# Halo sums on GpSimd, a claim per residual tile, idle matmuls in TensorE's planned waits, and new tune values, in a hybrid decoder block on eight cores

## The reference

```python
h = rmsnorm(x, norm_mix)
u_pool, u_rnn, u_gate, g_pool, g_rnn = split(h @ w_in)      # 512, 1024, 1024, 1024, 1024 columns
y_pool = (pool_mixer(u_pool) * scale) @ w_pool_out           # trailing windows 2/4/8/16, 4 groups of 128
v = causal_depthwise_conv(u_rnn, conv_w, conv_b)             # width 4: y_t = b + sum_k w[k] u_(t-3+k)
r, i = sigmoid(v @ w_a + b_a), sigmoid(v @ w_x + b_x)        # block-diagonal, 8 heads of 128
a = exp(-8 r softplus(-lam))
hr = scan(h_t = a_t h_(t-1) + sqrt(1 - a_t^2) i_t v_t)       # along the sequence
y_rnn = (hr * gelu(u_gate)) @ w_rnn_out
x = x + (sigmoid(g_pool) * y_pool + sigmoid(g_rnn) * y_rnn) @ w_o
g, u = split(rmsnorm(x, norm_ffn) @ w_ffn_in)                # 2816 each
out = rmsnorm(x + (silu(g) * u) @ w_ffn_out, norm_final)
```

## Time and profile before

| | us |
|---|---|
| median of 3 runs | 1113.86 |
| lowest and highest run | 1113.6, 1180.95 |
| the profiled execution | 1112.0 |
| its span, core 6 (slowest) | 1110.4 |
| even cores (role 0) | 1104.9 to 1110.4 |
| odd cores (role 1) | 1074.1 to 1080.5 |

### The profile page before, as it was taken

The page is one execution under the profiler, slowest core; times in us unless marked ns, Lnnn a source line. Parts: engine busy times, 40 slices in busy tenths (PEclk is TensorE's granted clock), DMA queues, the critical chain, the costliest instruction groups (busy, mean ns, idle before and its releaser), DMA issues.

```text
span 1110.4 us, 18573 instructions; the slowest of 8 cores (1074.1 to 1110.4 us)
## 1 busy us (share of the span) xinstructions
PE 995.2 (90%) x4720; PEld 444.9 (40%) x4720; DVE 727.9 (66%) x840; ACT 473.7 (43%) x602; POOL 257.5 (23%) x394
## 2 busy tenths in 40 slices
PE   3996679998879998798999999979999799999996
PEld 2442234443334443343444444434444344444442
DVE  4569777588997547987658989893633433334336
ACT  3476764256645216656228747761211110110112
...
GB/s 219 178 137 75 109 113 212 209 192 143 67 23 151 151 58 48 67 69 127 91 169 117 125 86 214 214 147 152 61 145 152 99 114 36 77 104 25 109 39 155
DMA packets 64914, 132.65 MB, mean 119 GB/s; under 512 B 7200, under 2 KB 11680, under 8 KB 64800
## 3 DMA queue, kind: packets, MB, share of 16 engines
...
...
## 4 chain that ended last, share of the span: by engine, by line
PE 72%; DVE 13%; issue 8%; ACT 4%; DMA 1%; POOL 1%; DVEq 0%; SPq 0%; ACTq 0%; POOLq 0%
PE ps L815 52%; PE ps L1160 13%; DVE f_v_f L857 4%; PE ps L1105 3%; PE ps L760 2%; PE ps L885 2%; DVE R_f L857 1%; DVE f_v_f L862 1%; DMA X<-x 1%; DVE R_f L941 1%; DVE f_w_f L928 1%; POOL rs_f L750 0%; PE ps L1029 0%; DVE ACW_f L857 0%; ACT hbt_f L744 0%
## 5 line engine op out<-in xcount | busy, mean ns | idle before, releaser
L815 PE MATMUL ps<-H_f,ring_f 128*128 128x512 bf16 x2816 | 649.0, 387 | 31.2 <-DVE uh_f L866 8.4
L815 PEld LDWEIGHTS ps<-H_f,ring_f 128*128 128x128 bf16 x2816 | 274.2, 99 | 385.9 <-issue 86.5
L1135 ACT ACTIVATE th_f<-ps 128x512 f32<-128x512 f32 (+1 forms) x66 | 48.7, 739 | 225.1 <-PE ps L815 220.0
L1160 PE MATMUL ps<-ACW_f 128*128 128x512 bf16 x528 | 116.4, 379 | 0.0
L676 POOL DMA_DIRECT2D ring_f<-w_ffn_in x88 | 47.3, 538 | 288.7 <-PE ps L815 244.0
L1139 DVE SCALAR_TENSOR_TENSOR th_f<-th_f,ps 128x512 f32<-128x512 f32 (+1 forms) x66 | 57.0, 864 | 80.0 <-ACT th_f L1135 62.7
L857 DVE SCALAR_TENSOR_TENSOR f_v_f<-ps,par,f_v_f 128x511 f32<-128x511 f32 (+5 forms) x90 | 89.6, 996 | 25.2 <-ACT f_v_f L852 16.6
L748 POOL TENSOR_SCALAR ms_f<-ms_f 128x1 f32<-128x1 f32 x64 | 23.5, 367 | 244.2 <-ACT hbt_f L744 241.6
L1045 ACT ACTIVATE th_f<-ps 128x512 f32<-128x512 f32 (+1 forms) x48 | 35.2, 738 | 101.8 <-PE ps L815 93.8
L1160 PEld LDWEIGHTS ps<-ACW_f 128*128 128x128 bf16 x528 | 51.4, 98 | 61.5 <-issue 0.4
L1166 DVE SCALAR_TENSOR_TENSOR X<-ps,X 128x1024 f32<-128x1024 f32 x36 | 43.9, 1223 | 41.9 <-PE ps L1160 37.3
...
## 6 DMA issues: line engine op xcount, KB each, us to landing
...
```

Source lines behind the costliest of these rows:

```text
L815: it.add(c_pe(n), lambda e, kc=kc, lo=lo, n=n, b=b: e.matmul(PS[pv.idx // 2][:, pv.idx % 2 + b, 0:n], lhsT=ring[:, w.idx, kc, :], rhs=src[ ...
L1135: it.add(c_act(U), lambda e, U=U, pg=pg, tv=tv: e.activation(out=two(th[:, tv.idx, 0:U], U), in_=P2(pg, U), func=AF.Tanh, scale=0.5), (pg, ...
L1160: it.add(c_pe(), lambda e, c=c, i=i: e.matmul(PS[pv.idx // 2][:, c, :], lhsT=acs[i][0](t * 128, (t + 1) * 128), rhs=WA[:, i, c * 512:(c + ...
```

## The change

Four edits:

1. The last three columns of u are now copied into `uh` by ScalarE, ahead of v = w3 u + b in the same item. When the units of four channel blocks of a segment are done with that, `halo_terms` computes on GpSimd, in three instructions for the four blocks, the three sums that the next segment's first three columns need (`hc`), from a table of taps in the parameters; the conv item of a later segment adds them in one VectorE instruction over 3 columns instead of three products.
2. A residual load of segment c1b claims the rows of R that its tile covers (two), and not all eight.
3. After the schedule is laid out, each TensorE item that starts a new PSUM value at least `keep` = 1.0 us after TensorE's last item (by the plan, and after 60 us) gets one matmul of 512 columns ahead of it, and one more per item of the chain that it waits for, at least 0.8 us apart, each waiting for that item's end. They write the PSUM bank of the item that follows, whose own first matmul starts the bank anew.
4. New tune values for both roles.

```diff
--- before.py
+++ after.py
@@ -32,16 +32,16 @@
         self.tune = tune
-TUNE0 = {"seq": "g0 g1 c01 g23 g45 c23 c45 g67 c67", "nc0": -3.85, "nc0s": 3.0, "step": 24.05, "gelu": 4.32,
-         "halo": 43.21, "pool": 25.05, "pools": 0.39, "t1": 93.39, "t1s": 1.88, "B0": 73.78, "S0": 285.6,
-         "B1": 386.59, "S1": -3.62, "B2": 589.89, "S2": 304.97, "ahead": 22.26, "c1": 1.278, "m": 37.56, "f": 7.53,
-         "u": 7.799, "slack": 0.098, "dev": 2, "hs": 20.8, "devt": 2, "pvo": 1, "pvt": 4, "pmo": 3, "pmt": 0,
-         "pbo": 0, "pbt": 2, "pao": 1, "pat": 0}
-TUNE1 = {"seq": "p0 p1 p23 g01 c01 p45 g23 c23 p67 g45 c45 g67 c67", "nc0": 11.68, "nc0s": 3.0, "step": 20.24,
-         "gelu": 3.77, "halo": 34.0, "pool": 45.93, "pools": 7.44, "t1": 183.82, "t1s": -0.44, "B0": 154.25,
-         "S0": 122.17, "B1": 334.63, "S1": -4.81, "B2": 394.66, "S2": 261.45, "ahead": -59.77, "c1": 0.565,
-         "m": 29.63, "f": 14.85, "u": 2.664, "slack": 0.121, "dev": 0, "hs": 20.01, "devt": 2, "pvo": 4, "pvt": 1,
-         "pmo": 1, "pmt": 0, "pbo": 4, "pbt": 0, "pao": 4, "pat": 3}
+TUNE0 = {"seq": "g0 g1 c01 g23 g45 c23 c45 g67 c67", "nc0": -1.38, "nc0s": 1.59, "step": 24.94, "gelu": 5.29,
+         "halo": 41.1, "pool": 24.03, "pools": 2.81, "t1": 98.04, "t1s": 3.77, "B0": 74.11, "S0": 276.71,
+         "B1": 384.25, "S1": -3.62, "B2": 668.36, "S2": 300.6, "ahead": 22.0, "c1": 1.249, "m": 37.56, "f": 7.38,
+         "u": 2.841, "slack": 0.086, "dev": 1, "hs": 20.8, "devt": 2, "pvo": 1, "pvt": 2, "pmo": 1, "pmt": 0,
+         "pbo": 0, "pbt": 0, "pao": 0, "pat": 0, "keep": 1.0}
+TUNE1 = {"seq": "p0 p1 p23 g01 c01 p45 g23 c23 p67 g45 c45 g67 c6 c7", "nc0": 11.68, "nc0s": -1.2, "step": 22.79,
+         "gelu": 1.4, "halo": 34.0, "pool": 47.28, "pools": 7.44, "t1": 236.41, "t1s": -0.44, "B0": 201.28,
+         "S0": 122.17, "B1": 334.63, "S1": -4.1, "B2": 394.66, "S2": 245.88, "ahead": -59.66, "c1": 0.611,
+         "m": 35.5, "f": 14.85, "u": 1.297, "slack": 0.121, "dev": 0, "hs": 21.04, "devt": 1, "pvo": 4, "pvt": 1,
+         "pmo": 0, "pmt": 0, "pbo": 2, "pbt": 0, "pao": 0, "pat": 1, "keep": 1.0}
 ROLES = (
     Role(0, (), 1024, ((1024,), (1024,)), (512, 512), 512, 5, (4, 4, 4, 4), (8, 8, 8, 8), (4, 2, 4, 2), True, 3, 4, True, TUNE0),
@@ -53,7 +53,8 @@
 C_CW, C_CB, C_BA, C_BX, C_LAM, C_PS, C_INV = 0, 32, 40, 48, 56, 64, 68
-C_N = 68 + 64
+C_HALO = 68 + 64
+C_N = C_HALO + 72
 class _Op:
@@ -498,6 +499,8 @@
         one_t = sb("one_t", [128, 1])
         hs_t = sb("hs_t", [128, 8])
         uh = sb("uh", [128, 8, 3])
+        hx = sb("hx", [128, 4, 3, 3])
+        hc = sb("hc", [128, 8, 3])
         ph = sb("ph", [128, 4, 16])
         hst = sb("hst", [128, 8])
         NSS = 8
@@ -602,14 +605,15 @@
         XR = R[:, :, :].rearrange("p k n -> p (k n)").bitcast(F32)
         ACP = PM[:, :, :].rearrange("p k n -> p (k n)")[:, 0:8 * NB].rearrange("p (m n) -> p m n", m=8)
-        RALL = [("R", j, q) for j in range(8) for q in range(2)]
+        RW = R[:, 0, :].shape[1]
         PALL = [("PM", j, q) for j in range(4) for q in range(2)]
         def xtile_of(seg, t):
             if seg != "c1b":
                 return (lambda: X[:, t * D:(t + 1) * D]), xtile(t), xtile(t)
-            return (lambda: XR[:, t * D:(t + 1) * D]), [("XR", t)], [("XR", t)] + RALL
+            return (lambda: XR[:, t * D:(t + 1) * D]), [("XR", t)], [("XR", t)] + [
+                ("R", j, q) for j in range(t * 2 * D // RW, -(-(t + 1) * 2 * D // RW)) for q in range(2)]
         def ac_of(seg, i):
@@ -837,6 +841,22 @@
         SQ = []
         gel = {}
+        halo_done = {}
+
+        def halo_terms(j0, p):
+
+            js = range(j0, j0 + 4)
+            mat = par[:, C_HALO + 9 * j0:C_HALO + 9 * j0 + 36].rearrange("p (j i m) -> p j i m", j=4, i=3)
+            it = Item("pool", p, "halo")
+            it.add(0.6, lambda e: e.tensor_tensor(
+                out=hx[:], in0=mat, in1=uh[:, j0:j0 + 4, :].unsqueeze(2).to_broadcast([128, 4, 3, 3]), op=ALU.mult),
+                [("uh", j) for j in js] + ["par"], ("hx",))
+            it.add(0.5, lambda e: e.tensor_tensor(out=hc[:, j0:j0 + 4, :], in0=hx[:, :, :, 0], in1=hx[:, :, :, 1],
+                                                  op=ALU.add), ("hx",), [("hc", j) for j in js])
+            it.add(0.5, lambda e: e.tensor_tensor(out=hc[:, j0:j0 + 4, :], in0=hc[:, j0:j0 + 4, :], in1=hx[:, :, :, 2],
+                                                  op=ALU.add), ("hx",), [("hc", j) for j in js])
+            G.put(it)
+
         def rnn_unit(seg, j, w, p):
             U = SEG[seg][1]
             tag = "r" + seg
@@ -849,6 +869,9 @@
             pu, v = psv(U), fval("v")
             hproj(pu, w, seg, p + T["u"], tag + ".u", also=(v, "rnnseq"), early=(seg == first and j == 0), contig=True)
             it = Item("act", p, tag + ".v0")
+            if seg != "c1b":
+                it.add(0.22, lambda e: e.activation(out=uh[:, j, :], in_=flat(pu, U)[:, U - 3:U], func=AF.Copy),
+                       (pu,), (("uh", j),))
             it.add(c_act(U, 2), lambda e: e.activation(out=F(v)[:, 0:U], in_=flat(pu, U), func=AF.Identity,
                                                        scale=cp(C_CW, 24 + j), bias=cp(C_CB, j)), (pu, "par"), (v,))
             G.put(it)
@@ -858,13 +881,13 @@
                     out=F(v)[:, d:U], in0=flat(pu, U)[:, 0:U - d], scalar=cp(C_CW, 8 * (3 - d) + j), in1=F(v)[:, d:U],
                     op0=ALU.mult, op1=ALU.add), (pu, "par"), (v,))
             if seg != first:
-                for d in (1, 2, 3):
-                    it.add(0.17, lambda e, d=d: e.scalar_tensor_tensor(
-                        out=F(v)[:, 0:d], in0=uh[:, j, 3 - d:3], scalar=cp(C_CW, 8 * (3 - d) + j),
-                        in1=F(v)[:, 0:d], op0=ALU.mult, op1=ALU.add), (("uh", j), "par"), (v,))
+                it.add(0.25, lambda e: e.tensor_tensor(out=F(v)[:, 0:3], in0=F(v)[:, 0:3], in1=hc[:, j, :], op=ALU.add),
+                       (("hc", j),), (v,))
+            G.put(it)
             if seg != "c1b":
-                it.add(0.17, lambda e: e.tensor_copy(out=uh[:, j, :], in_=flat(pu, U)[:, U - 3:U]), (pu,), (("uh", j),))
-            G.put(it)
+                halo_done.setdefault((seg, j // 4), []).append(j)
+                if len(halo_done[(seg, j // 4)]) == 4:
+                    halo_terms(j // 4 * 4, p)
             vb = Val("vb")
             if on_pool("pv", seg, j):
                 it = Item("pool", p, tag + ".vb")
@@ -1320,7 +1343,44 @@
                 else:
                     res.append(k)
             return res
+
+        idle = {}
+        KEEP = T.get("keep", 0.0)
+        prev = {}
+        last = None
+        begun = set()
         for it in order:
+            if it.eng == "pe":
+                pv = [v for v in it.ins[0][2] if isinstance(v, Val) and v.pool == "ps"]
+                t0 = last.end if last is not None else it.start
+                if KEEP and pv and id(pv[0]) not in begun and t0 > 60.0 and it.start - t0 >= KEEP:
+                    steps, cur, lim = [], it, it.start - 0.6
+                    while True:
+                        c = [w for w in cur.waits if w.dma is None] + ([prev[id(cur)]] if id(cur) in prev and cur is not it else [])
+                        c = [w for w in c if w.eng != "pe" and w.end > t0 + 0.5]
+                        if not c:
+                            break
+                        cur = max(c, key=lambda w: w.end)
+                        if cur.end <= lim:
+                            steps.append(cur)
+                            lim = cur.end - 0.8
+                    idle[id(it)] = (pv[0], steps[::-1])
+                begun.update(id(v) for v in pv)
+                last = it
+            prev[id(it)] = prev.get(it.eng)
+            if prev[id(it)] is None:
+                del prev[id(it)]
+            prev[it.eng] = it
+        done_by = {}
+        for it in order:
+            if id(it) in idle:
+                v, steps = idle[id(it)]
+                for w in [None] + steps:
+                    o = S.op("pe", lambda e, b=v.idx: e.matmul(PS[b // 2][:, b % 2, :], lhsT=ident[:], rhs=rga[:, 0:4, :],
+                                                               start=True, stop=True), ("ident", "rga"), phys([v]))
+                    if w is not None:
+                        o.deps.append(done_by[id(w)])
+                        done_by[id(w)].sig = True
             for fn, rd, wr in it.ins:
                 sem = it.dma
                 if sem == "ring":
@@ -1331,6 +1391,7 @@
                 def call(e, fn=fn, vals=[(v, v.idx) for v in it.vals]):
                     return fn(e)
                 o = S.op(it.eng, call, phys(rd), phys(wr), dma_sem=sem)
+                done_by[id(it)] = o
                 o.common = it.prio if it.tag in ("idn", "g1", "par") or any(it is x for x in XL[:TCOMMON]) else None
         S.finalize()
@@ -1465,6 +1526,11 @@
     base[:, C_BX:C_BX + 8] = chan(f(b_rg_x)[0])
```

(5 more changed lines are left out.)

## The result

The changed kernel takes 1071.46 us, the median of 4 runs (1070.5 to 1072.59), against 1113.86 before: a ratio of 0.962, 95% interval 0.9601 to 0.9639. That is 3.8% faster, 42.4 us, where 19 us had been forecast. Executions disturbed from outside are left out of every median and comparison here.

The account below looks back on a forecast made before the run. TensorE's own work, some 926 us, was taken as the floor in role 0, with waits and lower clock above it. Terms -6 - 11 - 4 + 3 = -18 took 1112.0 to 1094, adjusted to 1095 us; range 1074 to 1111.

Parts of the forecast that it names:

- Part 3: New tune values, reordering the plan and choosing engines: -4 us, bounds -15 and +11.
- Rival B: New order shortens role 0's first stage by 7 us, plus 5 us of middle waits: 1083 us, chance 0.23.
- Part 2: Halo terms of 32 conv items: one add replaces three small VectorE products, -11 us, bounds 3 and 15 us saved.
- five sixths: Share taken of the halo's 13.2 us on VectorE's side, since other waits stand close behind: 11 us.
- the copy: Halo copy of 159 ns, 32 times, moved to ScalarE: taken to cost there what VectorE is spared.
- Part 1: Claims per tile for the last segment's four residual loads: last add starts earlier, -6 us, bounds 0 and 7.5 saved.
- Both signs: Last residual add within 1.3 us of its matmuls; the 4.35 us wait before the last transposes below 2.
- Part 4: Idle matmuls ahead of waiting TensorE items: clock gain 4 us, delay 7, so +3 us; bounds -20 and +13.
- rival D: Idle matmuls pile up behind 24 waits for PSUM banks, costing 30 us in place of +3: 1122 us, chance 0.06.
- the band given as a sign: TensorE's mean granted clock was to stay within 0.01 of 0.969 if the forecast was right.
- Rival A: Idle matmuls hold TensorE's clock, -20 us in place of +3: 1072 us, mean clock 0.985 or more, chance 0.14.
- Rival C: Halo savings were hidden behind PSUM bank waits; halo and tune values give 3 us, not 15: 1107 us, chance 0.13.

Follow-up runs that it names:

- e4: Changed kernel's order and engine choices in role 0 and 1 with old halo work, old claims and no idle matmuls: 1092.77 us, 21.9 less than the kernel before.
- e14: Changed kernel's sequence alone, with old engines for products, casts and copies, old halo, old claims, no idle matmuls: 1110.24 us, 3.7 less than the kernel before.
- e6: Kernel before in its own order, with 20 products of role 0 moved from GpSimd to VectorE: 1113.53 us, 0.8 less than the kernel before.
- e5: Changed kernel in its own order, with 20 products of role 0 put back on GpSimd: 1078.35 us, 6.9 more than the changed kernel.
- e3: Changed kernel in its own order and engines, with the old halo work back: 1088.87 us, 17.4 more than the changed kernel.
- e7: Kernel before in its own order, with the new halo work and the new claims per tile: 1096.07 us, 18.3 less than the kernel before.
- e9: Changed kernel with three small VectorE products in place of the add, no GpSimd sums, copy kept on ScalarE: 1082.31 us, 10.9 more than the changed kernel.
- e10: Changed kernel with the copy back on VectorE behind the add, and GpSimd sums after the fourth conv item: 1075.83 us, 4.4 more than the changed kernel.
- e8: Kernel before in its own order, with the claims per tile alone: 1113.96 us, 0.4 less than the kernel before.
- e2: Changed kernel in its own order, with the four residual loads claiming all of R again: 1073.18 us, 1.7 more than the changed kernel.
- e1: Changed kernel without its idle matmuls, same plan, order and engines: 1071.49 us, a difference of 0.0 to the changed kernel.
- e15: Kernel before in its own order, with the idle matmuls alone: 1114.94 us, 1.0 more than the kernel before.

## Why the prediction was wrong

The direction held, and the profiles confirm the reading of what bounds the kernel: most of the gain is in TensorE's waits (those that the profile marks after the first 30 us, summed over an even core: 82 to 85 us before, 48 to 50 after, where 65 was forecast), the rest in less time at the lower clock, of which shorter waits leave less. The time fell 2.5 us outside the range, and by parts the working fares as follows.

**Part 3, the order: this is the step that failed.** "-4 us" stood against -21.9 measured (e4); the bound of -15 was passed too. The working costed the engine choices by their sums on VectorE and gave the order itself nothing of its own. The place was in the rows: from 120 to 150 us TensorE worked 18 of 30 us, in holes that end with steps of the recurrence. Rival B named that stage, but took a third of the 22 us that TensorE stands there and argued that its chain is ScalarE and VectorE work which the change doesn't remove. The chain needn't be removed. TensorE had other projections to do, later ones, and the new order puts them into the holes: VectorE is fuller than before (65.45 us of 69, 59.24 before), and TensorE is busy 14.5 us more beside it. B's 7 us for that stage were 10.7. But the sequence alone keeps only 3.7 us of this (e14); the other 18 come with the casts and products on other engines, which the working netted on VectorE as nearly nothing. An engine choice is no sum of durations: the 20 products cost nothing in one order (e6) and 6.9 us in another (e5). In e14 TensorE waits 7.1 us for GpSimd's casts, which is part of it; what makes up the rest stays open.

**Part 2, the halo: right in mechanism, a term mis-sized.** 11 us were forecast, 17.4 and about 18 measured in the two orders (e3, e7), above the upper bound of 15. The products alone gave the 11 us (10.9 in e9), so that term with its five sixths was right, though the long ones that it feared had no part in it in the new order. The term that failed is the copy, "it takes on the one engine what it gives on the other", zero: it gave 4.4 us (e10), and up to 2.1 us more together with the products. TensorE's waits for a bank did end with that copy, but its plain time on VectorE would explain most of the 4.4 us as well. The GpSimd sums took 0.5 us each on an engine busy 20%, and no VectorE add is marked as waiting for one; no run takes them away alone. Where the long products lay beside a GpSimd product, the rule of the Trainium skill, SBUF — State Buffer, on the shared port pair, had been read as a reason to discount the new add. With the products off GpSimd the add's mean is 169 ns, and 162 for the six adds into R; in e5, with them back, it is 203 and 437 ns:

```profile
L891 DVE TENSOR_TENSOR f_v_f<-f_v_f,hc_f 128x3 f32<-128x3 f32 x26 | 5.3, 203 | 2.7
L891 DVE TENSOR_TENSOR R_f<-R_f,hc_f 128x3 f32<-128x3 f32 x6 | 2.6, 437 | 0.6
```

The median stays at 163 ns in both kernels; single adds are caught, one for 1808 ns. Together that is 2.5 us more of VectorE's time (26 x 34 ns and 6 x 275 ns) in a run that is 6.9 us slower: it agrees with the rule, and it is a small part of the loss.

**Part 1, the claims: wrong reason.** "-6 us" stood against -0.4 in the old order (e8, not resolved) and -1.7 in the new one (e2). "It waits for its load, not for TensorE" was read from the issue times of the loads, and not from the row of the add itself, which has no wait marked at all: it came straight behind another VectorE instruction. Both signs that were to show the step right did come (the last add 0.2 us behind its matmuls, the wait before the last transposes 1.36 us), but not from the claims alone. The second came from the order, which puts all four adds ahead of the copies: e2 has a wait of 1.25 us there with the old claims. The first needs both: in e2 the last add starts 2.5 us behind its matmuls, and waits for its load. A sign that two causes can give proves neither.

**Part 4, the idle matmuls: next to nothing, where +3 was taken.** 0.0 us in the new order and +1.0 in the old (e1, e15). The mechanism fits: a small gain of clock (0.0035 of the mean, by estimate at most 4 us, as taken) against the matmuls' own time. Its price of a matmul at the lower clock, 0.43 us, is not what its row gives (2.72 / 7 = 0.39), which makes the 25 us there 21. That the clock isn't held was right, and rival D's pile stayed away: 29 matmuls on core 6, single or in pairs. The Trainium skill, TensorE: Matmul & The Clock Gate, Part 1, says that the clock drops after an idle stretch and comes back with activity. The rows of e1 agree, with a fall behind waits of 1.2 to 1.7 us; the reading "a little work keeps it up" they contradict. The clock's mean left the band given as a sign (0.981 to 0.991 for 0.969), without them as well.

Rival A named 1072 us, within 0.6 us of the result, for a reason that e1 and e15 refute; that is luck. Without e1 the profile would have seemed to confirm it, with the mean clock at 0.981 to 0.991 where A asked for 0.985.

**The sum** in the runs' own terms: -3.7 sequence (e14), -18.2 casts and products on other engines (e4), -17.4 halo (e3), -1.7 claims (e2), 0.0 idle matmuls (e1): -41 of the 42.4. It is one way of taking the parts; with the new halo the casts and products are worth 7.8 and not 18. Rival C (the halo hidden) fell with e7. No kernel of the study was faster than the changed one.
